# Closing one token tile four steps sooner, and the last inverse roots as one GpSimd power each, in a hybrid transformer block

## The chip, the cores and the metric

The kernel runs on one core of a Trainium2 chip. The metric is the device time of one execution in microseconds (us), the median of several. A core has TensorE (PE, matmuls), VectorE (DVE), ScalarE (ACT), GpSimd (POOL) and SyncE (SP, here only a queue that issues transfers). Each engine runs its own instructions in program order and waits on semaphores that the others raise.

## The reference, cut to what matters

512 tokens of width 1024 go through a gated block with attention and convolution, then through a retrieval layer over 16384 one-neuron experts, and a last layer norm. The change lies in the second half:

```python
# per token: 8 heads x 16 chosen experts with gates g
a = u_tab[experts] @ u2            # 128 dot products
y = sum(gelu(a) * g * v_tab[experts])
x = layer_norm(ALPHA * x + (1 + g2) * y, ln2_g, ln2_b)   # all in float32
```

## The kernel before

**Two ways for the tokens.** The tokens lie in four tiles of 128. For three of them (t = 0, 1, 2; TD = 3 of them) the gather over experts is done densely: for each of the CH = 128 groups of 128 experts, called steps here, PE multiplies a 128 x 384 matrix of weights by the group's 128 x 1024 rows of v_tab and sums in six PSUM banks (two halves of the width, three tiles). The fourth tile (t = TD) has its own 128 rows per token gathered by GpSimd's indirect transfers into a ring of 8 buffers (512 KB a row set), and DVE adds each to an accumulator in SBUF (`own_rows`, L1723). It has its own sum and norm (`own_sum`, `scales`).

**Split floats.** To keep float32 precision, every operand of PE is split into a high part (a copy by ACT in fp32r) and a low part (DVE's subtraction), and each product takes three matmuls. A step n is therefore this chain:

- SP loads rows of v (`load_v`) into one of DEEP = 5 buffers, once `low_v` of the step that had the buffer is done.
- ACT's `part_v(n)` makes the high part (L1039). The high parts have 5 buffers as well, so it waits for `v_mm`, the count of finished products, to reach n - 4 (product n-5 done). From step SIDE = 124 on the high and low parts lie elsewhere, in the space of the ring, and wait for the last own row only.
- DVE's `low_v(n)` makes the low part (L1688). DVE's `weigh(n)` makes the weights (L1676), ACT's `part_w(n)` their high part (L1026), DVE's `low_w(n)` their low part (L1683).
- PE's `second_product(n)` waits for `low_v(n)` and `low_w(n)`. It has 18 matmuls of 512 columns; from step 120 (CH - TAIL) only the 9 of the first half of the width. The 24 matmuls of each tile's second half for the last eight steps follow at the end, tile by tile.

**The order on DVE.** It is written out. In step n of the loop DVE does: `low_v` up to `low_target(n)`, then `weigh(n + 3)`, then as many own rows as OWN_AT[n] says, then `low_w(n + 2)`. ACT follows the same order with `part_v` and `part_w(n + 3)`. So `low_w(n + 2)`, for which PE waits, stands in DVE's queue behind every `low_v` of its step. The target is n + 4 until near the end:

```python
if n >= ROWS_TO + 2:
    return min(CH - 1, n + DEEP - 1 + (n - ROWS_TO - 1))
return n + DEEP - 1
```

`raw_target(n)` = `low_target(n)` + 5 tells SP how far to load. ROWS_TO, the step before which the own rows end, is 117 before the change. 98 of the 128 rows are spread evenly over the steps 46 to ROWS_TO - 1.

**The end.** DVE does `own_sum(0)` at the end of step 122, `own_sum(1)` at that of 124, and the norm of the own tile at that of 125. After the loop come, for each dense tile, `gated` (times the gate row, L1697), `last_sum` (L1704), statistics (L1106), `variances` (L1112, L1114), `centred` (L1139), the inverse root and `finished` (L1144). The inverse root is: ACT takes a square root (L797) while DVE does `centred`; then DVE takes the reciprocal and makes one Newton step (L1125 to L1129, five instructions), and for three of the tiles `shifts` (L1117). For the tiles TD and 1 the last operations go to others: ACT scales (L1075) and GpSimd adds the bias row (L777). GpSimd takes the first five inverse roots of the kernel as one power each (L682), at 11 us and between 374 and 392 us.

Of the kernel before, what the change touches and what calls it, by code (L numbers as in the profile page):

```python
# [9 lines left out]
ALU = mybir.AluOpType  # L10
ACT = mybir.ActivationFunctionType
# [6 lines left out]
TT = T // P  # L18
# [62 lines left out]
CH = NK  # L81
GR = 8
TD = TT - 1
# [28 lines left out]
TAIL = 8  # L112
# [6 lines left out]
W_STEP = BOTH - 5  # L119
GATE_STEP = BOTH + 5  # L120
EARLY_STEP = W_STEP // 2 + 2
ROWS_FROM, ROWS_EVEN, ROWS_TO = W_STEP, GATE_STEP + 5, CH - TAIL - 3
FIRST_ROWS = 4 * (BOTH - ROWS_FROM)
NORM_STEPS = tuple(range(DEEP_FROM + 9, DEEP_FROM + 21, 6))
XFIN_STEPS = tuple(range(DEEP_FROM + 21, DEEP_FROM + 21 + 6 * TT, 6))
# [45 lines left out]
def build(nc, x, ccol, w_modn, b_modc, w_modt, wblk, b_fc, conv_wc, conv_vec, keys_t, u_t, u_tab, v_tab, rows, out):  # L171
    with ExitStack() as ctx:
# [3 lines left out]
        def sb(name, shape, dt, kb):  # L176
            return nc.alloc_sbuf_tensor_at(name, shape, dt, offset=base + int(kb * KB))

        def sem(name):
            return ctx.enter_context(nc.semaphore(name))  # L180
# [58 lines left out]
        acc = sb("acc", [P, TT, D], F32, 184)  # L239
# [16 lines left out]
        xfin = sb("xfin", [P, TT, D], F32, 32)  # L256
        rows2 = sb("rows2", [P, 3, D], F32, 48)
# [7 lines left out]
        def small(name, shape, dt):  # L265
            n = 4
            for s in shape[1:]:
                n *= s
            t = nc.alloc_sbuf_tensor_at(name, shape, dt, offset=base + cur[0])
            cur[0] += (n + 31) // 32 * 32  # L270
            return t
# [11 lines left out]
        sq = small("sq", [P, 4, TT], F32)  # L283
# [49 lines left out]
        mask_r = sem("mask_r")  # L333
        cs_r = sem("cs_r")
        var_r = sem("var_r")
        dev_r = sem("dev_r")
        inv_r = sem("inv_r")
        xn_r = sem("xn_r")
        xT_mm = sem("xT_mm")
# [22 lines left out]
        xa_r = sem("xa_r")  # L362
# [4 lines left out]
        y_p = sem("y_p")  # L367
# [66 lines left out]
        class Chain:  # L434
# [5 lines left out]
            def link(self, ins):  # L440
                self.n += 1
                ins.then_inc(self.s, 1)
                self.eng.wait_ge(self.s, self.n)
# [42 lines left out]
        def w_parts(n):  # L486
            if O0 + 4 <= n < W0:
                return wo_hi[:, n - O0 - 4, :], wo_lo[:, n - O0 - 4, :]
            return (whi0, wlo0) if n == 0 else (whi[:, n % SPL, :], wlo[:, n % SPL, :])
# [179 lines left out]
        def _(pool):  # L669
# [102 lines left out]
                own_gather(j)  # L772

            pool.wait_ge(fin_in, 32)
            for i, t in enumerate((TD, 1)):
                pool.wait_ge(xa_r, 4 + i + 1)
                nc.gpsimd.tensor_tensor(xfin[:, t, :], acc[:, t, :], rows2[:, 2, :], ALU.add).then_inc(y_p, 1)  # L777


        @block.scalar  # L780
        def _(act):
            ch = Chain(act, ach)

            def hi(n):
# [6 lines left out]
                else:  # L791
                    need(act, blk_mm, n - SPL + 1 if n > SPL else 0)
                nc.scalar.activation(w_parts(n)[0][:, :], raw[:, s % RAW, :], ACT.Copy).then_inc(blk_hi, 1)

            def root(done, ts=slice(0, TT)):
                act.wait_ge(var_r, 5 + done)
                nc.scalar.activation(sq[:, 1, ts], sq[:, 0, ts], ACT.Sqrt).then_inc(dev_r, 1)  # L797

            def modulated(sh, sc, first, biased):

# [28 lines left out]
            for n in range(G0):  # L829
# [19 lines left out]
                elif n < V0 and (n - C0) % 2 == 1:  # L849
                    i = (n - C0) // 2  # L850
# [32 lines left out]
            for h in range(HEADS):  # L883
                n = G0 + 2 * h
# [79 lines left out]
            def part_u(c):  # L964
                act.wait_ge(u_in[c % RAW], 16 * (c // RAW + 1))
                need(act, u_mm, c - SPL + 1)
                nc.scalar.activation(whi[:, c % SPL, :], raw[:, c % RAW, :], ACT.Copy).then_inc(u_hi, 1)  # L967

            def gelu(c):
                m = c // 4  # L970
                act.wait_ge(u_mm, c + 1)
                if c >= SPILL + GS:
                    act.wait_ge(w_mul, c - SPILL - GS + 1)
                elif c == SPILL + PS:
                    act.wait_ge(sel_r, TT)
                elif c < SPILL + PS and c % 4 == 0 and m > 1:
                    act.wait_ge(gel_out[m % 2], 16 * (m // 2))
                nc.scalar.activation(gel_slot(c), bank[c % 2][:, 0:TN], ACT.Gelu_apprx_tanh).then_inc(gel_r, 1)
# [63 lines left out]
            for j in range(FILL):  # L1042
                ahead(SPILL + j)
                i = j - FIRST_W
# [9 lines left out]
            for n in range(CH):  # L1054
                if PRE + n - 1 < CH:
                    gelu(PRE + n - 1)
                if PRE + n + 2 < CH:
                    part_u(PRE + n + 2)
                while high_next <= low_target(n):
                    part_v(high_next)  # L1060
                    high_next += 1
                if n + 3 < CH:
                    part_w(n + 3)
                if n in (EARLY_STEP, W_STEP):
                    part = slice(0, SLOTS // 2) if n == EARLY_STEP else slice(SLOTS // 2, SLOTS)
                    act.wait_ge(dot_r, part.stop)
                    nc.scalar.activation(own_a[:, part], own_a[:, part], ACT.Gelu_apprx_tanh).then_inc(own_gel, 1)
                if n == CH - 3:
                    root(1, slice(TD, TT))
            for i, t in enumerate((TD, 0, 1, 2)):  # L1070
                if i:
                    root(1 + i, slice(t, t + 1))
                if t in (TD, 1):
                    act.wait_ge(scale_r, 4 + i)
                    nc.scalar.activation(acc[:, t, :], acc[:, t, :], ACT.Copy,  # L1075
                                         scale=sq[:, 2, t:t + 1]).then_inc(xa_r, 1)
# [3 lines left out]
        def _(dve):  # L1080
            ch = Chain(dve, dch)
            link = ch.link
            done = [0]
# [36 lines left out]
            def scales(last, roots, ts, meanwhile, shift=True):  # L1120

                variances(last, ts)
                link(meanwhile())
                dve.wait_ge(dev_r, roots)
                link(nc.vector.reciprocal(sq[:, 2, ts], sq[:, 1, ts]))  # L1125
                link(nc.vector.tensor_tensor(sq[:, 3, ts], sq[:, 2, ts], sq[:, 2, ts], ALU.mult))
                link(nc.vector.tensor_tensor(sq[:, 3, ts], sq[:, 3, ts], sq[:, 0, ts], ALU.mult))
                link(nc.vector.tensor_scalar(sq[:, 3, ts], sq[:, 3, ts], -0.5, 1.5, ALU.mult, ALU.add))
                link(nc.vector.tensor_tensor(sq[:, 2, ts], sq[:, 2, ts], sq[:, 3, ts], ALU.mult))  # L1129
                if shift:  # L1130
                    shifts(ts)

# [4 lines left out]
            def centred(dst, src, rows_of, t):  # L1137

                return nc.vector.scalar_tensor_tensor(out=dst[:, t, :], in0=src[:, t, :], scalar=mv[:, t, 0:1],  # L1139
                                                      in1=rows_of[:, 1, :], op0=ALU.subtract, op1=ALU.mult)  # L1140
# [106 lines left out]
            for n in range(G0):  # L1247
# [20 lines left out]
                elif n < V0 and (n - C0) % 2 == 1:  # L1268
                    i = (n - C0) // 2
# [34 lines left out]
            for h in range(HEADS):  # L1304
                n = G0 + 2 * h
# [394 lines left out]
            def last_sum(t, half):  # L1700

                cut = slice(half * HALF, (half + 1) * HALF)
                dve.wait_ge(pv_add, TD * half + t + 1)
                link(nc.vector.scalar_tensor_tensor(out=xfin[:, t, cut], in0=xfin[:, t, cut], scalar=ALPHA,  # L1704
                                                    in1=acc[:, t, cut], op0=ALU.mult, op1=ALU.add))
                return bn(xfin, t, half)
# [34 lines left out]
            for j in range(FILL):  # L1741
                low_u(SPILL + j + 2)
                i = j - FIRST_W
# [13 lines left out]
            for n in range(CH):  # L1757
                if PRE + n + 2 < CH:
                    low_u(PRE + n + 2)
                while low_next <= low_target(n):  # L1760
                    low_v(low_next)
                    low_next += 1
                if n + 3 < CH:
                    weigh(n + 3)
                for _ in range(DOT_AT[n]):
                    dot(next(dots))
                own_rows(n)
                if n + 2 < CH:
                    low_w(n + 2)
                if n in (EARLY_STEP + 1, W_STEP + 1):  # L1770
                    own_weights(int(n > W_STEP))
                if n == GATE_STEP:
                    dve.wait_ge(u_mm, CH)
                    diagonals(dg2, 40)
                if n == GATE_STEP + 3:
                    gate_row(rows2[:, 0, :], 0, 2)
                if n == CH - 6:
                    dve.wait_ge(fin_in, 32)
                    dve.wait_ge(x1_in, 16 * TT)
                    own_sum(0)  # L1780
                if n == CH - 4:
                    own_last = own_sum(1)
                if n == CH - 3:
                    scales(own_last, 1, ts=slice(TD, TT), meanwhile=lambda: centred(acc, xfin, rows2, TD))
            for t in range(TD):
                gated(t, 0)
            for t in range(TD):
# [1 line left out]

            for t in range(TD):  # L1790
                gated(t, 1)
                scales(last_sum(t, 1), 2 + t, shift=t < TD - 1, ts=slice(t, t + 1),
                       meanwhile=lambda: centred(acc, xfin, rows2, t))
                if t == 0:
                    finished(xfin, acc, rows2, t).then_inc(y_r, 1)
# [414 lines left out]
```

## Time and profile before

| | |
|---|---|
| median of 3 runs | 1601.46 us (1601.44 to 1603.22) |
| profiled execution | 1601.95 us |
| its span | 1600.1 us |
| PE busy | 1554.0 us (97%) |
| DVE busy | 1360.2 us (85%) |
| mean granted TensorE clock | 0.994 |

Busy is the time in which an engine worked on an instruction. Matmuls overlap, so a busy PE need not be at its peak. The span goes from the first to the last instruction on the core. The last 30 us of it hold the end of the loop, PE's three last groups of matmuls and the norms.

### The profile page before, as it was taken

The numbers are of one execution on the slowest core, as the hardware profiler recorded it, in microseconds if no ns is written. First come the engines' busy times: TensorE is split into PE (matmuls) and PEld (weight loads), VectorE is DVE, ScalarE is ACT, GpSimd is POOL, SyncE is SP. The second block draws the span as 40 slices with busy tenths as digits, with TensorE's granted clock in tenths as the row PEclk, the third lists the DMA queues.
The fourth block names the chain that finished last, engine by engine and source line by source line (L and its number), as shares of the span: only waits on it lengthen the run. The fifth ranks groups of instructions, "written<-read, shape, count | busy, mean of one in ns | idle before, by whom it ended". The sixth has DMA issues, their size and how long they took to land.

```text
span 1600.1 us, 21502 instructions
## 1 busy us (share of the span) xinstructions
PE 1554.0 (97%) x7776; PEld 1360.0 (85%) x7776; DVE 1360.2 (85%) x2580; ACT 677.4 (42%) x918; POOL 677.1 (42%) x451
## 2 busy tenths in 40 slices
PE   7999999997999999999999999999999999999996
PEld 4888777776899999999999999999998888878885
DVE  6579888696288899979994799999998899989988
ACT  4334656534433345554554433333333433333341
POOL 0201000001042878778764576666673344434401
PEclk9999999998999999999999999999999999999999
DMA  8423343562366666676778999999999999999961
GB/s 357 146 91 120 131 131 122 195 200 104 111 239 225 168 171 175 159 217 178 203 191 265 388 410 409 410 394 390 391 355 344 375 406 411 410 412 410 411 260 53
DMA packets 159753, 421.64 MB, mean 264 GB/s; under 512 B 31264, under 2 KB 64160, under 8 KB 159136
## 3 DMA queue, kind: packets, MB, share of 16 engines
q1 hardware_dynamic: 69552, 263.91, 44.7%
q0 software_dynamic: 57200, 139.58, 25.2%
q10 hardware_dynamic: 32896, 16.78, 3.8%
q8 instruction: 62, 1.02, 0.3%
q14 instruction: 43, 0.35, 0.1%
HBM read 375.03 MB, written 45.15 MB: 263 GB/s over the span
## 4 chain that ended last, share of the span: by engine, by line
PE 74%; DVE 19%; DMA 4%; issue 2%; ACT 1%; SPq 0%; DVEq 0%; POOL 0%; ACTq 0%
PE bank L1806 23%; PE bank L1808 23%; PE bank L1807 23%; DMA vraw<-in_v_tab_dram 3%; DVE one L1650 2%; DVE one L1648 2%; DVE wlo L1485 2%; DVE one L1652 2%; PE bank L1957 1%; PE bank L1942 1%; PE bank L2101 1%; PE bank L2077 1%; DMA modn<-in_w_modn_dram 1%; DVE eq L1588 1%; DVE acc L1723 1%
## 5 line engine op out<-in xcount | busy, mean ns | idle before, releaser
L1806 PE MATMUL bank<-act_hi,whi 128*128 128x384 f32 (+1 forms) x1352 | 481.2, 356 | 2.3 <-DVE act_lo L1207 1.5
L1807 PE MATMUL bank<-act_lo,whi 128*128 128x384 f32 (+1 forms) x1352 | 472.2, 349 | 0.0
L1808 PE MATMUL bank<-act_hi,wlo 128*128 128x384 f32 (+1 forms) x1352 | 472.1, 349 | 0.0
L1806 PE MATMUL bank<-vhi,eh 128*128 128x512 f32 x768 | 299.8, 390 | 3.8 <-DVE el L1683 3.7
L1808 PE MATMUL bank<-vhi,el 128*128 128x512 f32 x768 | 299.7, 390 | 0.0
L1807 PE MATMUL bank<-vlo,eh 128*128 128x512 f32 x768 | 299.7, 390 | 0.0
L1806 PEld LDWEIGHTS bank<-act_hi,whi 128*128 128x128 f32 x1352 | 255.1, 189 | 19.6 <-DVE act_lo L1207 2.1
L744 POOL DMA_INDIRECT gates_by_key<-selW,selS x128 | 238.3, 1862 | 69.3 <-issue 44.5
L1807 PEld LDWEIGHTS bank<-act_lo,whi 128*128 128x128 f32 x1352 | 255.2, 189 | 13.7
L1808 PEld LDWEIGHTS bank<-act_hi,wlo 128*128 128x128 f32 x1352 | 254.7, 188 | 13.4
L767 POOL DMA_INDIRECT ring<-in_v_tab_dram,idxN x128 | 168.8, 1319 | 203.0 <-DVE acc L1723 186.4
L728 POOL DMA_INDIRECT ring<-in_u_tab_dram,idxN x128 | 186.5, 1457 | 102.9 <-DVE ring L1490 59.6
L1688 DVE TENSOR_TENSOR vlo<-vraw,vhi 128x1024 fp32r<-128x1024 f32 x128 | 156.1, 1222 | 43.4 <-ACT vhi L1039 41.3
L1039 ACT ACTIVATE vhi<-vraw 128x1024 fp32r<-128x1024 f32 x128 | 135.2, 1058 | 127.6 <-PE bank L1808 114.7
L1485 DVE TENSOR_TENSOR wlo<-raw,whi 128x1024 fp32r<-128x1024 f32 x108 | 131.7, 1220 | 67.4 <-ACT whi L967 66.8
L1026 ACT ACTIVATE eh<-wf 128x384 fp32r<-128x384 f32 x128 | 67.4, 526 | 272.4 <-DVE wf L1676 272.4
L1806 PEld LDWEIGHTS bank<-vhi,eh 128*128 128x128 f32 x768 | 144.3, 188 | 34.9 <-issue 6.2
L1808 PEld LDWEIGHTS bank<-vhi,el 128*128 128x128 f32 x768 | 144.2, 188 | 30.2
L1807 PEld LDWEIGHTS bank<-vlo,eh 128*128 128x128 f32 x768 | 144.2, 188 | 29.3 <-issue 0.2
L1723 DVE SCALAR_TENSOR_TENSOR acc<-ring,own_a,acc 128x1024 f32<-128x1024 f32 x127 | 162.6, 1280 | 4.4
L1490 DVE SCALAR_TENSOR_TENSOR ring<-ring,x2s 128x1024 f32<-128x1024 f32 x128 | 150.0, 1219 | 4.1 <-DMA ring<-in_u_tab_dram,idxN 4.1
L967 ACT ACTIVATE whi<-raw 128x1024 fp32r<-128x1024 f32 x128 | 134.6, 1053 | 3.0 <-DMA raw<-in_u_t_dram 3.0
(256 smaller groups left out, 1903.3 us busy)
## 6 DMA issues: line engine op xcount, KB each, us to landing
raw<-in_u_t_dram SPq DMA_DIRECT2D x128, 512.0 KB, 7.1
vraw<-in_v_tab_dram SPq DMA_DIRECT2D x128, 512.0 KB, 9.7
raw<-in_wblk_dram SPq DMA_DIRECT2D x61, 512.0 KB, 4.4
gring<-gates_by_key SPq DMA_DIRECT2D x32, 768.0 KB, 12.4
raw<-in_w_modt_dram SPq DMA_DIRECT2D x32, 512.0 KB, 3.7
gates_by_key<-stage ACTq DMA_DIRECT2D x8, 2048.0 KB, 13.9
gelu_ahead<-gelz SPq DMA_DIRECT2D x20, 768.0 KB, 4.2
gback<-gelu_ahead SPq DMA_DIRECT2D x20, 768.0 KB, 17.1
```

Of the source, the lines that this page charges most:

```text
L728: pool.indirect_dma_start(out=ring[:, j % RING, :], out_offset=None, in_=u_tab, in_offset=bass.IndirectOffsetOnAxis(ap=idxN[:, j:j + 1], a ...
L744: pool.indirect_dma_start(out=gates_flat, out_offset=bass.IndirectOffsetOnAxis(ap=selS[:, n:n + 1], axis=0), in_=selW[:, n:n + 1], in_offs ...
L767: pool.indirect_dma_start(out=ring[:, j % RING, :], out_offset=None, in_=v_tab, in_offset=bass.IndirectOffsetOnAxis(ap=idxN[:, j:j + 1], a ...
L967: nc.scalar.activation(whi[:, c % SPL, :], raw[:, c % RAW, :], ACT.Copy).then_inc(u_hi, 1)
L1039: nc.scalar.activation(v_parts(n)[0], row, ACT.Copy).then_inc(v_hi, 1)
L1485: nc.vector.tensor_tensor(wlo[:, c % SPL, :], raw[:, c % RAW, :], whi[:, c % SPL, :].bitcast(F32), ALU.subtract).then_inc(u_lo, 1)
L1490: nc.vector.scalar_tensor_tensor(out=ring[:, j % RING, :], in0=ring[:, j % RING, :], scalar=1.0, in1=x2s[:], op0=ALU.mult, op1=ALU.mult, a ...
L1688: nc.vector.tensor_tensor(low, v_row(n)[0], high.bitcast(F32), ALU.subtract).then_inc(v_lo, 1)
L1723: nc.vector.scalar_tensor_tensor(out=acc[:, TD, :], in0=ring[:, j % RING, :], scalar=own_a[:, j:j + 1], in1=acc[:, TD, :], op0=ALU.mult, o ...
L1806: mm(o, wh, mh, start=start, stop=False)
L1807: mm(o, wh, ml, start=False, stop=False)
L1808: return mm(o, wl, mh, start=False, stop=stop)
```

## The change

ROWS_TO goes from CH - TAIL - 3 = 117 to 113. With it move the steps over which the own rows are spread (98 rows in 67 steps, not 71) and, through `low_target` and `raw_target`, the steps in which DVE, ACT and SP run further ahead: `low_target` is now 120, 122, 124, 126, 127 for the steps 115 to 119, where it was 119 to 122 for 115 to 118 and 124, 126, 127 for 119 to 121. `own_sum` is done in the steps 115 and 117 (122 and 124 before) and the own norm in 119 (125 before). The last four inverse roots are one GpSimd power each; ACT's square roots and DVE's five instructions are gone.

```diff
-ROWS_FROM, ROWS_EVEN, ROWS_TO = W_STEP, GATE_STEP + 5, CH - TAIL - 3
+ROWS_FROM, ROWS_EVEN, ROWS_TO = W_STEP, GATE_STEP + 5, CH - TAIL - 7
+OWN_SUMS, OWN_NORM = (ROWS_TO + 2, ROWS_TO + 4), ROWS_TO + 6
...
-            for i, t in enumerate((TD, 1)):
-                pool.wait_ge(xa_r, 4 + i + 1)
-                nc.gpsimd.tensor_tensor(xfin[:, t, :], acc[:, t, :], rows2[:, 2, :], ALU.add).then_inc(y_p, 1)
+            for i, t in enumerate((TD, 0, 1, 2)):
+                inverse_root(6 + i, slice(t, t + 1))
+                if t in (TD, 1):
+                    pool.wait_ge(xa_r, 4 + i // 2 + 1)
+                    nc.gpsimd.tensor_tensor(xfin[:, t, :], acc[:, t, :], rows2[:, 2, :], ALU.add).then_inc(y_p, 1)
...
-            def root(done, ts=slice(0, TT)):
-                act.wait_ge(var_r, 5 + done)
-                nc.scalar.activation(sq[:, 1, ts], sq[:, 0, ts], ACT.Sqrt).then_inc(dev_r, 1)
...
-                if n == CH - 3:
-                    root(1, slice(TD, TT))
             for i, t in enumerate((TD, 0, 1, 2)):
-                if i:
-                    root(1 + i, slice(t, t + 1))
...
                 variances(last, ts)
                 link(meanwhile())
-                dve.wait_ge(dev_r, roots)
-                link(nc.vector.reciprocal(sq[:, 2, ts], sq[:, 1, ts]))
-                link(nc.vector.tensor_tensor(sq[:, 3, ts], sq[:, 2, ts], sq[:, 2, ts], ALU.mult))
-                link(nc.vector.tensor_tensor(sq[:, 3, ts], sq[:, 3, ts], sq[:, 0, ts], ALU.mult))
-                link(nc.vector.tensor_scalar(sq[:, 3, ts], sq[:, 3, ts], -0.5, 1.5, ALU.mult, ALU.add))
-                link(nc.vector.tensor_tensor(sq[:, 2, ts], sq[:, 2, ts], sq[:, 3, ts], ALU.mult))
+                dve.wait_ge(inv_r, roots)
...
-                if n == CH - 6:
+                if n == OWN_SUMS[0]:
                     dve.wait_ge(fin_in, 32)
                     dve.wait_ge(x1_in, 16 * TT)
                     own_sum(0)
-                if n == CH - 4:
+                if n == OWN_SUMS[1]:
                     own_last = own_sum(1)
-                if n == CH - 3:
-                    scales(own_last, 1, ts=slice(TD, TT), meanwhile=lambda: centred(acc, xfin, rows2, TD))
+                if n == OWN_NORM:
+                    scales(own_last, 6, ts=slice(TD, TT), meanwhile=lambda: centred(acc, xfin, rows2, TD))
```

## Rows read from the trace of the kernel before

**Rows 1.** The page, busy time of each engine; then its group of own row additions.

```profile
PE 1554.0 (97%) x7776; PEld 1360.0 (85%) x7776; DVE 1360.2 (85%) x2580; ACT 677.4 (42%) x918; POOL 677.1 (42%) x451
...
L1723 DVE SCALAR_TENSOR_TENSOR acc<-ring,own_a,acc 128x1024 f32<-128x1024 f32 x127 | 162.6, 1280 | 4.4
```

**Rows 2.** The timeline of PE: start us, us, [idle before <-releaser]; products 92, 122, 123, last matmul.

```profile
1439.04 0.47 PE L1806 MATMUL bank<-vhi,eh 128*128 128x512 f32 x1 [1.01 <-DVE el L1683]
...
1558.48 0.47 PE L1806 MATMUL bank<-vhi,eh 128*128 128x512 f32 x1 [0.84 <-DVE el L1683]
...
1561.71 0.47 PE L1806 MATMUL bank<-vhi,eh 128*128 128x512 f32 x1 [0.94 <-DVE el L1683]
...
1588.15 0.39 PE L1808 MATMUL bank<-vhi,el 128*128 128x512 f32 x1
```

**Rows 3.** The timeline of ACT: high parts of v 122, then of 123 and 124.

```profile
1545.49 1.06 ACT L1039 ACTIVATE vhi<-vraw 128x1024 fp32r<-128x1024 f32 x1 [0.15 <-PE bank L1808]
...
1549.58 2.01 ACT L1039 ACTIVATE vhi<-vraw 128x1024 fp32r<-128x1024 f32 x2 [0.74 <-PE bank L1808]
```

**Rows 4.** The timeline of DVE, steps 119 to 125.

```profile
1550.67 2.36 DVE L1688 TENSOR_TENSOR vlo<-vraw,vhi 128x1024 fp32r<-128x1024 f32 x2 [1.92 <-ACT vhi L1039]
...
1555.04 2.36 DVE L1688 TENSOR_TENSOR vlo<-vraw,vhi 128x1024 fp32r<-128x1024 f32 x2 [1.07 <-ACT vhi L1039]
1557.31 0.55 DVE L1676 TENSOR_TENSOR wf<-gback,gring 128x384 f32<-128x384 f32 x1
...
1559.40 1.23 DVE L1688 TENSOR_TENSOR vlo<-vraw,vhi 128x1024 fp32r<-128x1024 f32 x1 [1.07 <-ACT vhi L1039]
...
1562.64 0.69 DVE L1731 TENSOR_TENSOR acc<-acc,rows 128x512 f32<-128x512 f32 x1
...
1564.70 0.54 DVE L1676 TENSOR_TENSOR wf<-gback,gring 128x384 f32<-128x384 f32 x1
...
1569.30 0.20 DVE L1112 BATCH_NORM_AGGREGATE mv<-stats 128x2 f32<-128x12 f32 x1
...
1569.61 1.27 DVE L1139 SCALAR_TENSOR_TENSOR acc<-xfin,mv,rows 128x1024 f32<-128x1024 f32 x1
...
1571.88 0.16 DVE L1117 SCALAR_TENSOR_TENSOR sq<-mv,sq 128x1 f32<-128x1 f32 x1
```

**Rows 5.** The timeline of DVE after the loop.

```profile
1573.75 2.57 DVE L1704 SCALAR_TENSOR_TENSOR xfin<-xfin,acc 128x512 f32<-128x512 f32 x1
...
1590.47 0.68 DVE L1697 TENSOR_TENSOR acc<-bank,rows 128x512 f32<-128x512 f32 x1
...
1592.95 2.27 DVE L1139 SCALAR_TENSOR_TENSOR acc<-xfin,mv,rows 128x1024 f32<-128x1024 f32 x1
...
1596.23 1.42 DVE L1144 SCALAR_TENSOR_TENSOR xfin<-acc,sq,rows 128x512 f32<-128x512 f32 x2
```

**Rows 6.** The timeline of GpSimd after the loop: its two bias additions.

```profile
1573.38 2.39 POOL L777 TENSOR_TENSOR xfin<-acc,rows 128x1024 f32<-128x1024 f32 x1 [50.25 <-ACT acc L1075]
...
1591.81 2.34 POOL L777 TENSOR_TENSOR xfin<-acc,rows 128x1024 f32<-128x1024 f32 x1 [16.04 <-ACT acc L1075]
```

**Rows 7.** Two powers on the timeline of GpSimd, and what DVE did during the second.

```profile
374.16 0.72 POOL L682 TENSOR_TENSOR sq<-sq,power 128x2 f32<-128x2 f32 x1 [89.00 <-DVE sq L1429]
...
384.95 1.66 POOL L682 TENSOR_TENSOR sq<-sq,power 128x2 f32<-128x2 f32 x1 [4.74 <-DVE sq L1429]
```

```profile
384.78 2.47 DVE L1416 SCALAR_TENSOR_TENSOR outg<-xres,mv,rows 128x1024 f32<-128x1024 f32 x2
```

**Rows 8.** Busy by window (PE, PEld, DVE, ACT, POOL, PEclk, DMA share, GB/s); DMA issues, KB, us to landing.

```profile
1400.00:1440.00 40.00, 38.87 (x170) 31.60 (x170) 35.46 (x42) 13.52 (x18) 15.79 (x13) 1.00 1.02 411
```

```profile
vraw<-in_v_tab_dram SPq DMA_DIRECT2D x9, 512.0 KB, 16.3
```

```profile
gring<-gates_by_key SPq DMA_DIRECT2D x32, 768.0 KB, 12.4
...
gback<-gelu_ahead SPq DMA_DIRECT2D x20, 768.0 KB, 17.1
```

More of the change, by code:

```diff
@@ L335, in build @@
         var_r = sem("var_r")
-        dev_r = sem("dev_r")
         inv_r = sem("inv_r")
@@ L1791, in _ @@
                 gated(t, 1)
-                scales(last_sum(t, 1), 2 + t, shift=t < TD - 1, ts=slice(t, t + 1),
+                scales(last_sum(t, 1), 7 + t, shift=t < TD - 1, ts=slice(t, t + 1),
                        meanwhile=lambda: centred(acc, xfin, rows2, t))
```

## The prediction

> **What bounds the kernel now.** I read the page first: PE is busy for 97% of the span [rows 1]. So time is won or lost where PE pauses, and after its last matmul. The waits of PE in the last 300 us are three, all for `low_w` on DVE (the instruction "el"): 1.01 us at 1439 us, before product 92, and 0.84 and 0.94 before the products 122 and 123 [rows 2]. Next the timelines of ACT and DVE, to see what stands ahead of "el". ACT starts the high part of v 122 at 1545.49 and that of 123 at 1549.58, each released by PE [rows 3]: one product takes 4.08 us, and the buffers of the high parts are the leash between PE and ACT. Last, the end: the last matmul starts at 1588.15 [rows 2] and DVE takes up its result only at 1590.47 [rows 5], 2.32 us later. A matmul (0.39 us) and a handover (0.1) make 0.49, so DVE is 1.83 us behind PE there; from 1559.40 on DVE has work nearly without a gap. The last 30 us are partly DVE's. Over the steps 46 to 116 the transfers are at their limit, too: the window at 1400 has the DMA engines busy all the time, at 411 GB/s, and a v load takes 16.3 us to land [rows 8].
>
> **What moves away from the end.** Two `own_sum` of 2.06 us (1562.64 to 1564.70) and a norm of 2.66 us (1569.30 to 1571.88 and 0.08 more) [rows 4] leave steps in which DVE is late, 6.8 us in all. That could win at most what DVE is behind at the end, 1.83 us, and little of PE's pauses: those before products 122 and 123 come from `low_v` in the steps 120 and 121, not from the sums.
>
> **What moves with ROWS_TO: the look-ahead.** This is the part that decides. `low_target` jumps by two from step 116 on. In step 116 DVE must do `low_v(121)` and `low_v(122)` before `low_w(118)`. ACT's `part_v(122)` waits for product 117 to end. But product 118 can't start without `low_w(118)`. So PE is idle from the end of 117 until a whole chain has run. In the kernel before, the same `low_v(122)` was in step 118, where `low_w(118)` had long been done, and the first pair (123, 124) was in step 119, behind which only `low_w(121)` stood. The chain in pieces, all from rows: product's last start to ACT's start 0.26; ACT's start to DVE's 1.09 (1549.58 [rows 3] to 1550.67 [rows 4]); a pair of `low_v` 2.27 (1555.04 to 1557.31), one of them 1.14; `weigh` to PE 1.17 (1557.31 [rows 4] to 1558.48 [rows 2]), of which 0.47 is `weigh`.
>
> - Product 118: 0.26 + 1.09 + 1.14 + 1.17 = 3.66 us of pause.
> - Product 119: step 117 has 123, which waits for product 118, and then 124. 0.26 + 1.09 + 2.27 + 1.17 = 4.79.
> - Product 120: `own_sum(1)` stands at the end of step 117, a pair in 118. From the start of `low_w(119)`: 0.47 + 2.06 + 2.27 + 1.17 = 5.97, against 0.70 + 4.08 = 4.78 at which PE is done with 119. Pause 1.19.
> - Product 121: PE's products are now half as long (2.04). From `weigh(121)` to `low_v(127)` is 2.09 (1557.31 to 1559.40 [rows 4]), then 1.14 and 1.17: 4.40, against 0.47 + 0.70 + 2.04 = 3.21. Pause 1.19.
> - Product 122: the own norm is at the end of step 119. With the norm at 2.26 (below): 0.47 + 2.26 + 0.05 + 1.17 = 3.95, against 2.74. Pause 1.21.
>
> Sum 12.04 us. Before, the pauses before 122 and 123 are 1.01 and 1.11 (the idle shown is 0.17 less each, since a matmul lasts 0.39 and the next may start after 0.23), and one before 125 is some 0.13: 2.25. All later `low_w` are ready in time. PE's last matmul comes 9.79 us later, at 1597.94. No pause is bridged: ACT, too, stands in `part_v` and nothing else feeds PE.
>
> **The inverse roots.** The power of 128 x 2 takes 0.72 us alone, but 1.66 when DVE had just begun an operation with two inputs in SBUF (384.78): it ended about 0.56 after DVE's first of the two [rows 7]. `centred` is such an operation, and it starts right behind the variance, so the power will come behind it. Before, `centred` to `shifts` is 2.27 us (1569.61 to 1571.88 [rows 4]). Then: 1.27 + 0.56 + 0.04 = 1.87. So a norm gains 0.40 us, not the 0.97 of the five instructions; bounds 0 (as now) and 0.97 (power hidden). The Trainium skill (SBUF — State Buffer, Who interferes with whom) says that a VectorE instruction with two SBUF inputs and a GpSimd one that reads SBUF exclude each other for the whole instruction. The rows agree; by it a norm gains 0.40 and the sum below stands, with the power at 0.72 alone it would be 0.6 less.
>
> The same is seen the other way round: GpSimd's addition (2.39 us from 1573.38, [rows 6]) stretches a 0.69 us sum on DVE to 2.57 [rows 5], to 0.55 after GpSimd's end, and the other (to 1594.15) stretches the last `centred` from 1.27 to 2.27. ACT's square root is on no path, and its removal is worth nothing: it lies under `centred`, which hides it.
>
> **The end of the span.** DVE is free when PE's last matmul ends, so the last `gated` starts at 1597.94 + 0.49 = 1598.43, 7.96 us later than before. From the last `centred` to `finished` it was 3.28 (1592.95 to 1596.23 [rows 5]), now 1.87: 1.41 won. But tile 1 now ends 5.44 us ahead of tile 2 (24 matmuls of 0.227), at 1592.99. Its `centred` starts 2.48 later (as 1590.47 to 1592.95), its scale is there after 1.87, and GpSimd adds 1.50 after that (1571.88 [rows 4] to 1573.38 [rows 6]): 1598.84. The last `last_sum` is due 0.7 after its `gated`, at 1599.14, falls into the addition and is held to 0.55 after 1601.23: 1.9 us lost. If it wins the race, the last `centred` is held instead, for 1.1. Bounds 0 and 1.9; I take 1.8. Span: + 7.96 - 1.41 + 1.8 = + 8.3 us.
>
> **The rows packed closer.** A step moves 512 KB of v, 192 KB each of gates and of saved gelus (768 KB in four steps [rows 8]), and 98/71 = 1.38 own rows of 512 KB (128 x 1024 floats [rows 1]): 1.64 MB, 402 GB/s at 4.08 us. With 98/67 = 1.46 rows it is 1.68 MB, 413 GB/s. The DMA engines give 411. The kernel before is close already: product 92 came 1.01 us late [rows 2], behind a v load, after the loads of x and of the norm's rows in the steps 54 to 84. By step 90 the new spread wants 3 more rows (65, not 62), 1.57 MB or 3.8 us of transfer, and 0.5 more by step 113. The end gives none of it back to PE. DVE's own load grows with it (0.08 rows of 1.28 us [rows 1]) and stays under 4.08. Bounds: 0, where the buffers take it, and 5 us. I take 3.3, since the buffers had nothing left at product 92, but some elsewhere.
>
> **Sum.** + 8.3 + 3.3 = + 11.6 us on the span of 1600.1. The profiled execution took 1601.95, 0.5 above the median of 1601.46; on the median it is 1613.1, 0.7% slower. One measurement of this kernel tells some 0.2% (3.2 us) from no change.
>
> **Rivals.**
>
> - *Only the look-ahead costs* (25%): the buffers swallow the denser rows. For it: one wait of 1 us in 290 us before; gathers have 8 buffers. Against it: 413 over 411. 1601.5 + 8.3 = 1609.8.
> - *The transfers cost in full or more* (20%): v loads arrive late again and again, and DVE, with only 0.16 us a step to spare, doesn't catch up. 1601.5 + 8.3 + 5 to 7 = 1615 to 1617.
> - *Faster* (5%): the pauses of 118 and 119 don't arise, as if `part_v(122)` didn't have to wait. Then the freed DVE wins its 1.83 and the 0.13 before product 125, and 1.41 of the root; with the late addition of GpSimd up to 1.8 lost: 1598.1 to 1599.9. And if the pauses before 122 and 123 went as well, 1596. It decides only if the new pauses together stay under some 3.5 us instead of 12; the release of that cast by PE is plain in [rows 3], which speaks against it.
> - *No change* (5%): pauses of 118 and 119 half as long and no transfer cost: 1601 to 1604.
> - My forecast has the rest, 45%; its own range is 1611 to 1615.
>
> All but one tenth is slower by more than 0.2%. The range that leaves two in ten out is 1607 to 1618: the look-ahead without GpSimd's collision and without transfers (+ 6), and with both in full.
>
> **What the new profile would show.** PE idle by some 3.5 and 4.6 us before products 118 and 119, released by "el", and three pauses near 1 us behind them; the cast of v 122 still released by PE; the power ending some 0.5 us after `centred`; the last `last_sum` or `centred` on DVE held by GpSimd's addition; and, in the steps 70 to 112, several PE waits for "el" behind v loads of 18 us and more. The prediction is wrong if PE runs through 118 and 119, or if the waits in the middle are absent or many times larger.

## The result, and the profile after

The changed kernel takes 1615.55 us (median of 4 runs, 1613.87 to 1616.35), against 1601.45 for the kernel before beside it: ratio 1.0088, 95% interval 1.0076 to 1.0099, so 14.1 us slower. The forecast was 1613.1, range 1607 to 1618. The profiled execution took 1615.5, its span is 1613.7 us, 13.6 more than before. In two of the experiments below one execution fell into a slow state (2232.18 us in experiment 2, 1733.01 in experiment 5); the ratios leave these two out.

In the changed kernel L1795 to L1797 are the matmuls, L1037 and L1677 the high and low part of v, L1665, L1024 and L1672 `weigh` and the high and low part of the weights. The timeline of PE (start us, duration us, idle us before and its releaser) shows ten pauses from step 46 on, all released by the low part of the weights. Six of them:

```profile
1390.45 0.47 PE L1795 MATMUL bank<-vhi,eh 128*128 128x512 f32 x1 [1.09 <-DVE el L1672]
...
1441.90 0.47 PE L1795 MATMUL bank<-vhi,eh 128*128 128x512 f32 x1 [1.27 <-DVE el L1672]
...
1552.74 0.76 PE L1795 MATMUL bank<-vhi,eh 128*128 128x512 f32 x1 [3.49 <-DVE el L1672]
...
1563.13 0.77 PE L1795 MATMUL bank<-vhi,eh 128*128 128x512 f32 x1 [4.63 <-DVE el L1672]
...
1571.62 0.47 PE L1795 MATMUL bank<-vhi,eh 128*128 128x512 f32 x1 [0.75 <-DVE el L1672]
...
1574.82 0.47 PE L1795 MATMUL bank<-vhi,eh 128*128 128x512 f32 x1 [0.88 <-DVE el L1672]
```

The third and the fourth are the products 118 and 119, which ran without a pause before. What stood ahead of their weights is seen on the timelines of ACT and DVE:

```profile
1549.34 1.06 ACT L1037 ACTIVATE vhi<-vraw 128x1024 fp32r<-128x1024 f32 x1 [3.02 <-PE bank L1797]
...
1558.60 2.00 ACT L1037 ACTIVATE vhi<-vraw 128x1024 fp32r<-128x1024 f32 x2 [5.91 <-PE bank L1797]
```

```profile
1550.43 1.22 DVE L1677 TENSOR_TENSOR vlo<-vraw,vhi 128x1024 fp32r<-128x1024 f32 x1 [2.81 <-ACT vhi L1037]
1551.57 0.55 DVE L1665 TENSOR_TENSOR wf<-gback,gring 128x384 f32<-128x384 f32 x1
1552.04 0.55 DVE L1672 TENSOR_TENSOR el<-wf,eh 128x384 fp32r<-128x384 f32 x1
1559.68 2.36 DVE L1677 TENSOR_TENSOR vlo<-vraw,vhi 128x1024 fp32r<-128x1024 f32 x2 [7.09 <-ACT vhi L1037]
1561.96 0.55 DVE L1665 TENSOR_TENSOR wf<-gback,gring 128x384 f32<-128x384 f32 x1
1562.43 0.55 DVE L1672 TENSOR_TENSOR el<-wf,eh 128x384 fp32r<-128x384 f32 x1
```

Read together: PE ends product 117 and releases the cast of v 122 (1549.34); DVE makes its low part (1550.43), then `weigh(119)`, then `low_w(118)` (1552.04), and PE starts product 118 at 1552.74. The same once more with a pair, 123 and 124, for product 119. The engines take turns: DVE is idle for 7.09 us while PE makes product 118 and ACT the cast that waited for it, then PE is idle while DVE makes two low parts and the weights. In the kernel before the cast of v 122 was followed by low weights that PE needed only much later [rows 3, 4].

The cast of v 122 also shows the middle of the kernel: it is at 1549.34, not 1545.49 [rows 3]. It is 3.85 us late before any of the tail's pauses.

The first matmul of each of the two products takes 0.76 and 0.77 us. The view by windows shows why (PE busy, PEld, DVE, ACT, POOL, the granted clock, DMA share, GB/s):

```profile
1549.00:1552.70 3.70, 0.25 (x2) 0.00 (x0) 2.16 (x3) 1.58 (x2) 0.00 (x0) 0.95 0.38 131
1552.70:1554.00 1.30, 1.26 (x3) 1.10 (x4) 0.00 (x0) 0.00 (x0) 0.00 (x0) 0.50 0.80 280
1554.00:1556.00 2.00, 2.00 (x6) 1.57 (x6) 0.00 (x0) 0.00 (x0) 0.00 (x0) 0.57 1.04 413
1556.00:1558.60 2.60, 2.50 (x11) 1.69 (x9) 0.00 (x0) 0.00 (x1) 0.00 (x0) 1.00 0.83 338
1558.60:1563.10 4.50, 0.00 (x0) 0.00 (x1) 3.42 (x5) 2.55 (x4) 0.00 (x0) 0.94 0.01 2
1563.10:1564.50 1.40, 1.37 (x3) 1.16 (x4) 1.33 (x3) 1.40 (x2) 0.00 (x0) 0.50 0.00 0
```

By the end of each pause the granted clock had gone to 0.50, the lower of its two levels (1.2 GHz, the other is 2.4), and it stayed there for about 3 us of matmuls (to 1555.8 in the first case). Product 118 took 5.60 us and 119 took 5.53 (from a product's first matmul to where the next product's would start, 0.23 after the last), where 4.08 is usual: 3.0 us that no step of the forecast has.

At the end, PE's last matmul, then the timelines of DVE and GpSimd:

```profile
1603.26 0.39 PE L1797 MATMUL bank<-vhi,el 128*128 128x512 f32 x1
```

```profile
1603.68 0.69 DVE L1686 TENSOR_TENSOR acc<-bank,rows 128x512 f32<-128x512 f32 x1 [0.89 <-PE bank L1797]
1604.41 2.54 DVE L1693 SCALAR_TENSOR_TENSOR xfin<-xfin,acc 128x512 f32<-128x512 f32 x1
...
1608.02 1.27 DVE L1128 SCALAR_TENSOR_TENSOR acc<-xfin,mv,rows 128x1024 f32<-128x1024 f32 x1
1609.81 1.41 DVE L1133 SCALAR_TENSOR_TENSOR xfin<-acc,sq,rows 128x512 f32<-128x512 f32 x2 [0.52 <-POOL sq L682]
```

```profile
1604.06 2.34 POOL L779 TENSOR_TENSOR xfin<-acc,rows 128x1024 f32<-128x1024 f32 x1 [1.53 <-ACT acc L1069]
1608.18 1.51 POOL L682 TENSOR_TENSOR sq<-sq,power 128x1 f32<-128x1 f32 x1 [1.78 <-DVE sq L1108]
```

GpSimd's addition begins 0.35 us ahead of DVE's last sum, which takes 2.54 us, not 0.69. The power ends 0.4 us behind `centred`, and DVE is idle for 0.52. From `centred` to `finished` it is 1.79 us, not 3.28 [rows 5].

### The profile page after: what moved, and what is told of

The parts are those of the page before. It is cut to its first block, busy times and chain, and to the rows that moved or that the text cites. A ratio compares the mean times of both kernels' runs of the same rounds, so it can differ in the third digit from the quotient of the medians.

```text
span 1613.7 us, 21481 instructions
## 1 busy us (share of the span) xinstructions
PE 1559.8 (97%) x7776; PEld 1363.1 (84%) x7776; DVE 1356.3 (84%) x2560; ACT 672.5 (42%) x913; POOL 687.7 (43%) x455
## 4 chain that ended last, share of the span: by engine, by line
PE 75%; DVE 17%; DMA 4%; issue 2%; ACT 1%; POOL 0%; SPq 0%; POOLq 0%; DVEq 0%; ACTq 0%
PE bank L1795 23%; PE bank L1797 23%; PE bank L1796 23%; DMA vraw<-in_v_tab_dram 3%; DVE one L1639 2%; DVE one L1637 2%; DVE wlo L1474 2%; DVE one L1641 2%; PE bank L2090 1%; PE bank L1946 1%; DVE acc L1712 1%; PE bank L1931 1%; PE bank L2066 1%; DMA modn<-in_w_modn_dram 1%; DVE wf L1665 1%
## 5 line engine op out<-in xcount | busy, mean ns | idle before, releaser
L1795 PE MATMUL bank<-act_hi,whi 128*128 128x384 f32 (+1 forms) x1352 | 482.1, 357 | 2.3 <-DVE act_lo L1196 1.5
L1797 PE MATMUL bank<-act_hi,wlo 128*128 128x384 f32 (+1 forms) x1352 | 473.2, 350 | 0.0
L1795 PE MATMUL bank<-vhi,eh 128*128 128x512 f32 x768 | 301.9, 393 | 14.1 <-DVE el L1672 13.9
L1797 PE MATMUL bank<-vhi,el 128*128 128x512 f32 x768 | 301.0, 392 | 0.0
L1795 PEld LDWEIGHTS bank<-act_hi,whi 128*128 128x128 f32 x1352 | 255.8, 189 | 19.6 <-DVE act_lo L1196 2.1
L1797 PEld LDWEIGHTS bank<-act_hi,wlo 128*128 128x128 f32 x1352 | 255.1, 189 | 13.4
L767 POOL DMA_INDIRECT ring<-in_v_tab_dram,idxN x128 | 173.9, 1359 | 185.6 <-DVE acc L1712 167.1
L1677 DVE TENSOR_TENSOR vlo<-vraw,vhi 128x1024 fp32r<-128x1024 f32 x128 | 156.1, 1221 | 51.8 <-ACT vhi L1037 50.8
L1037 ACT ACTIVATE vhi<-vraw 128x1024 fp32r<-128x1024 f32 x128 | 134.7, 1054 | 128.5 <-PE bank L1797 113.6
L1024 ACT ACTIVATE eh<-wf 128x384 fp32r<-128x384 f32 x128 | 67.4, 526 | 286.6 <-DVE wf L1665 286.6
L1795 PEld LDWEIGHTS bank<-vhi,eh 128*128 128x128 f32 x768 | 145.1, 189 | 47.9 <-issue 19.1
L1797 PEld LDWEIGHTS bank<-vhi,el 128*128 128x128 f32 x768 | 144.8, 189 | 30.3
## 6 DMA issues: line engine op xcount, KB each, us to landing
gring<-gates_by_key SPq DMA_DIRECT2D x32, 768.0 KB, 11.8
gates_by_key<-stage ACTq DMA_DIRECT2D x8, 2048.0 KB, 14.1
```

The source lines that it names most:

```text
L767: pool.indirect_dma_start(out=ring[:, j % RING, :], out_offset=None, in_=v_tab, in_offset=bass.IndirectOffsetOnAxis(ap=idxN[:, j:j + 1], a ...
L1037: nc.scalar.activation(v_parts(n)[0], row, ACT.Copy).then_inc(v_hi, 1)
L1677: nc.vector.tensor_tensor(low, v_row(n)[0], high.bitcast(F32), ALU.subtract).then_inc(v_lo, 1)
L1795: mm(o, wh, mh, start=start, stop=False)
L1797: return mm(o, wl, mh, start=False, stop=stop)
```

## The experiments

All ratios are against the kernel before, run on the same chip; its medians were 1600.65 us for experiments 1, 2, 4 and 5, 1601.05 for 3, 6, 7 and 8, and 1601.54 for 9 to 11.

**1. The look-ahead alone**, in the kernel before:

```diff
-    if n >= ROWS_TO + 2:
-        return min(CH - 1, n + DEEP - 1 + (n - ROWS_TO - 1))
+    if n >= 115:
+        return min(CH - 1, n + DEEP - 1 + (n - 114))
```

> The kernel before with nothing but the look-ahead moved: it begins at step 115, the own rows still end at 117, sums and norm stay in the steps 122 to 125. Theory (the look-ahead makes PE wait for a high part that waits for PE): product 118 waits some 3.7 us plus the two own rows that stand ahead of its low weights in step 116 (2.6), product 119 4.8, product 121 1.2; both long pauses are followed by slow products (1.4 us each, as in the profile after), and the 2.2 us of pauses before 122 and 123 and DVE's 1.8 us of lag at the end are absorbed: about 10 to 11 us, 1611 to 1612.5. Rival (the look-ahead is harmless, it is the sums and the norm put between the low parts that stop PE): no sum stands there in this kernel, so 1601 to 1602.

Measured: 1612.45 us, ratio 1.0071 (1.0058 to 1.0084), 11.8 us slower than 1600.65. The two pauses are there, the first longer by the two own rows that DVE does ahead of `low_w(118)`:

```profile
1551.96 0.77 PE L1806 MATMUL bank<-vhi,eh 128*128 128x512 f32 x1 [6.08 <-DVE el L1683]
...
1562.88 0.73 PE L1806 MATMUL bank<-vhi,eh 128*128 128x512 f32 x1 [4.63 <-DVE el L1683]
```

The two products behind them took 6.13 and 5.80 us, 3.8 us above the usual. So the look-ahead by itself stops PE; no sum or norm has been moved here. The rival falls.

**2. The rows closer, alone**, in the kernel before:

```diff
-          + spread(SLOTS - FIRST_ROWS - ROWS_EVEN + BOTH, n, ROWS_EVEN, ROWS_TO) for n in range(CH)]
+          + spread(SLOTS - FIRST_ROWS - ROWS_EVEN + BOTH, n, ROWS_EVEN, ROWS_TO - 4) for n in range(CH)]
```

> The kernel before with nothing but the own rows spread over the steps 46 to 112; look-ahead, sums and roots as before. Theory (transfers at their limit): PE waits more often for low weights in the steps 70 to 95, the cast of v 122 comes 3 to 4 us later than 1545.49, and 1604.5 to 1605.5 in all. Rival (the buffers take it, and the late cast in the profile after has another cause): 1601 to 1602.

Measured: 1605.22 us, ratio 1.0027 (1.0017 to 1.0037), 4.6 us by the medians, 4.3 by the ratio. PE has five pauses between 1390 and 1492, the longest 1.55 us, where it had one. The cast of v 122 is at 1549.12, 3.63 late:

```profile
1549.12 1.06 ACT L1039 ACTIVATE vhi<-vraw 128x1024 fp32r<-128x1024 f32 x1 [0.73 <-PE bank L1808]
```

**3. The same with lighter transfers.** Experiment 2, and of the saved gelus only the first of each four loaded (the engines' work stays as it is; the output isn't the reference's):

```diff
-                sp.dma_start(gback[:, q % 3], gel_dram[m]).then_inc(back_in[q % 3], 16)
+                sp.dma_start(gback[:, q % 3, 0:1], gel_dram[m, :, 0:1]).then_inc(back_in[q % 3], 16)
...
-                    src = gback[:, q % 3, c % 4, :]
+                    src = gback[:, q % 3, 0, :]
```

> The kernel before with the own rows closer, and with a quarter of the bytes of the saved gelus loaded (48 KB a step, not 192; all four steps of a group use the same quarter, so the output is not the reference's; the work of the engines is the same). Theory (the 4.6 us of the denser rows are transfer time): 1.54 MB a step are 377 GB/s, nothing waits for transfers, and the pause of 1 us of the kernel before goes too: 1599 to 1600.5. Rival (DVE with 31 steps of two rows, not 27, is what is late): 1604 to 1605.

Measured: 1598.85 us, ratio 0.9988 (0.9979 to 0.9997). All pauses of the middle are gone, those of the kernel before too; the two that are left in the trace after 1240 us are before products 122 and 123. In the same window as [rows 8], and the time a v load takes in it:

```profile
1400.00:1440.00 40.00, 40.00 (x178) 33.11 (x178) 38.29 (x45) 15.75 (x20) 19.66 (x16) 1.00 1.01 389
```

```profile
vraw<-in_v_tab_dram SPq DMA_DIRECT2D x10, 512.0 KB, 6.7
```

DVE has the same denser rows and is busier in this window than before (38.29 us against 35.46), and nothing is late. In the changed kernel a v load there takes 17.6 us. So the price of the denser rows is that of transfers, not of DVE's work.

**4. The powers alone**, in the kernel before:

```diff
-                dve.wait_ge(dev_r, roots)
-                link(nc.vector.reciprocal(sq[:, 2, ts], sq[:, 1, ts]))
...
+                dve.wait_ge(inv_r, roots)
...
+                inverse_root(6 + i, slice(t, t + 1))
```

> The kernel before with nothing but the last four inverse roots as GpSimd powers. Theory (a power has to wait until centred has let go and ends 0.5 us behind it, so each norm gains 0.4): all four norms lie in a stretch in which DVE is behind, 1.6 us in all, 1599.9. Rival A (the power is hidden, 0.97 per norm, of which 1.83 and 0.97 count): 1598.6. Rival B (GpSimd's addition for tile 1 is in its queue ahead of the last power and holds it up): 1601.5 or more.

Measured: 1598.83 us, ratio 0.9992 (0.9983 to 1.0), by the medians 1.8 us faster; the interval only just reaches no change. Each power takes 1.5 us and ends 0.4 us behind `centred`, near the 0.56 of the forecast. The last one stands in the queue behind GpSimd's addition and costs nothing by it, for `centred` is held up by the same addition.

**5. The changed kernel with its look-ahead back at step 119**:

```diff
-    if n >= ROWS_TO + 2:
-        return min(CH - 1, n + DEEP - 1 + (n - ROWS_TO - 1))
+    if n >= 119:
+        return min(CH - 1, n + DEEP - 1 + (n - 118))
```

> The changed kernel with the look-ahead alone put back to step 119. Theory: PE runs through 118 and 119, the pauses before 122 and 123 are back. Rows closer + 3.8, DVE no longer behind - 1.8 - 0.1, last root - 1.4, collision with GpSimd's addition + 1.8: 1603.7. Rival (the sums in the steps 115 to 119 are what stops PE): 1612 to 1615.

Measured: 1605.16 us, ratio 1.0025 (1.0016 to 1.0034). PE runs through 118 and 119. Against its own kernel before it is 4.0 us (by the ratio) to 4.5 us slower, where the terms of the expectation add up to 2.3. The trace shows 1.05 us of that: the pause before product 122 is 1.89 us, not 0.84, because the own norm, now at the end of step 119, holds up the pair of step 120. The rest is within the interval of the ratio.

```profile
1561.96 0.47 PE L1795 MATMUL bank<-vhi,eh 128*128 128x512 f32 x1 [1.89 <-DVE el L1672]
```

**6. The pauses filled.** The changed kernel, PE kept at work in them:

```diff
             def second_product(n, halves):
+                for _ in range({118: 17, 119: 22}.get(n, 0)):
+                    mm(bank[0][:, 0:P], ident[:], consts[:], start=True, stop=True)
                 pe.wait_ge(v_lo, n + 1)
```

> The changed kernel with matmuls into a bank that nobody reads put ahead of PE's waits for products 118 and 119 (17 and 22 of 128 x 128 in float32). The pauses stay, but PE isn't idle in them. If the slow first matmuls of 118 and 119 (1.4 us each beyond 4.08) come from the granted clock that fell in the idle, they go, and the pause before product 120, which they had covered, comes back with 1.2: 1.6 us less, 1613.9, and the clock is at 1.0 in the window from 1550 to 1566. Rival (they are slow for another reason, such as a transfer or an operand that is late): the time stays at 1615.5.

Measured: 1613.55 us, ratio 1.0082 (1.0069 to 1.0096), against 1.0088 of the changed kernel; as a difference of times that is not settled. The trace settles it: PE starts the extra matmuls at 1548.15, and product 118 at 1551.86, 3.71 later, as in the changed kernel (3.65). But the clock is at its upper level and the product takes 4.22 us, not 5.60:

```profile
1548.15 3.96 PE L2116 MATMUL bank<-consts,ident 128*128 128x128 f32 x34
1551.86 0.48 PE L1795 MATMUL bank<-vhi,eh 128*128 128x512 f32 x1
...
1556.08 5.07 PE L2116 MATMUL bank<-consts,ident 128*128 128x128 f32 x44
1560.90 0.48 PE L1795 MATMUL bank<-vhi,eh 128*128 128x512 f32 x1
...
1566.13 0.47 PE L1795 MATMUL bank<-vhi,eh 128*128 128x512 f32 x1 [0.88 <-DVE el L1672]
```

```profile
1551.00:1553.00 2.00, 2.00 (x15) 1.82 (x15) 0.66 (x2) 0.52 (x1) 0.00 (x0) 1.00 0.64 176
1553.00:1556.00 3.00, 3.00 (x15) 2.47 (x14) 0.00 (x0) 0.00 (x0) 0.00 (x0) 1.00 1.03 410
```

The last row of the first fence is product 120: its pause is back (0.88 us of idle). The slow clock of product 119 had hidden it. From the cast of v 122 to the end of the span it is 64.4 us in the changed kernel (1549.34 to 1613.7) and 63.0 here (1548.41 on ACT's timeline to 1611.4): 1.4 us, near the 1.6 expected.

**7. Tile 1's last operation on DVE**, in the changed kernel, ACT's scaling and GpSimd's addition for that tile taken out:

```diff
-                if t == 0:
+                if t < TD - 1:
                     finished(xfin, acc, rows2, t).then_inc(y_r, 1)
...
-                if t in (TD, 1):
+                if t == TD:
                     pool.wait_ge(xa_r, 4 + i // 2 + 1)
```

> The changed kernel with tile 1's last operation done by DVE in one instruction, as for tile 0, not by ACT's scaling and GpSimd's addition. Theory (the addition locks DVE's last_sum out for 1.85 us): that goes, and DVE's 1.28 us lie in the 0.9 us in which it waits for PE, so 0.3 to 0.4 are lost: 1.5 us less, 1614. Rival (the sum was late for another reason): 1615.5 to 1616.

Measured: 1612.6 us, ratio 1.0070 (1.0057 to 1.0084), 2.9 us less than the changed kernel by the ratios, where 1.5 was expected; the intervals of the two overlap a little. In the trace the last sum takes 0.69 again, and from the last `gated` to the end of the span it is 8.2 us (1606.02 to 1614.2), where it was 10.0:

```profile
1606.02 0.68 DVE L1686 TENSOR_TENSOR acc<-bank,rows 128x512 f32<-128x512 f32 x1
1606.74 0.69 DVE L1693 SCALAR_TENSOR_TENSOR xfin<-xfin,acc 128x512 f32<-128x512 f32 x1
```

The profiled execution was the slowest of the five, 1615.97 us, and it shows something more. PE pauses before 118 and 119 just as long as in the changed kernel (3.50 and 4.63 us), and this part of the program is the same, but matmuls stay at the slow pace of one in 0.43 us for 5.6 and 4.3 us, not 3. The two products take 6.78 and 6.18 us: 4.8 us above the usual, not 3.0. Product 118's last matmul, 119's first, and one that is still slow 3.5 us later:

```profile
1560.36 0.40 PE L1797 MATMUL bank<-vhi,el 128*128 128x512 f32 x1
1565.38 0.77 PE L1795 MATMUL bank<-vhi,eh 128*128 128x512 f32 x1 [4.63 <-DVE el L1672]
...
1568.93 0.63 PE L1797 MATMUL bank<-vhi,el 128*128 128x512 f32 x1
```

So what the slow clock costs behind the same pause differs from one execution to the next.

**8. The first sum early.** Rows (117) and look-ahead (119) as before, powers, and

```diff
+OWN_SUMS, OWN_NORM = (ROWS_TO, CH - 6), CH - 3
```

> A version meant to be faster: rows and look-ahead as in the kernel before (117, 119), own_sum(0) in step 117, where DVE waits for casts in the next two steps, own_sum(1) and the norm in 122 and 125 as late work, and the powers. Theory: no pause of PE is added; DVE catches up with PE before the last tile (- 1.8 - 0.1), the last root gives 1.4, and GpSimd's addition takes 1.8 back: 1599.2. Rival (any sum ahead of low parts costs PE its length): 1601 or more.

Measured: 1599.62 us, ratio 0.9991 (0.9982 to 1.0), 1.4 us faster where the terms of the expectation add up to 1.5; the interval only just reaches no change. As expected, no pause of PE is added in steps 117 to 127, DVE waits 0.88 us for PE at the last tile, and the last sum takes 2.54 us under GpSimd's addition.

**9. Experiments 7 and 8 together.**

> The version with the first sum in step 117, and tile 1's last operation on DVE as well. Theory (GpSimd's addition holds DVE's last sum for 1.85 us, and DVE's own instruction for it costs 0.2 after the 0.9 us in which it waits for PE): 1.6 us below the version with the first sum alone, about 3 us below the kernel before. Rival (the collision cost nothing at the end): 0.2 us above the version with the first sum alone.

Measured: 1597.37 us, ratio 0.9978 (0.9969 to 0.9987), 3.5 us by the ratio and 4.2 by the medians, faster than the kernel before by more than the noise. About 3 were expected.

**10. Weights first.** Experiment 9 with the look-ahead taken out and, from step 117 on, DVE's order turned round; sums in the steps 117 and 118, norm in 119:

```diff
-    if n >= ROWS_TO + 2:
-        return min(CH - 1, n + DEEP - 1 + (n - ROWS_TO - 1))
-    return n + DEEP - 1
+    return min(CH - 1, n + DEEP - 1)
...
-                while low_next <= low_target(n):
+                while n < ROWS_TO and low_next <= low_target(n):
                     low_v(low_next)
                     low_next += 1
...
                 if n + 2 < CH:
                     low_w(n + 2)
+                while low_next <= low_target(n):
+                    low_v(low_next)
+                    low_next += 1
```

> Rows until step 116 as in the kernel before, no look-ahead beyond n + 4 at all, and from step 117 on DVE does weigh and low_w ahead of low_v; sums in 117 and 118, own norm in 119, powers, tile 1's last operation on DVE. Theory (what stops PE is that its weights stand behind low parts it doesn't need yet): no pause of PE after step 117, so the 2.25 us before products 122, 123 and 125 go, DVE's lag of 1.8 goes, the last root gives 1.4, the tile 1 change costs 0.2: 5.3 us below before. Rival (the look-ahead is needed, since DVE has 2.08 us of work for a product of 2.04 and ACT's casts come in between): new pauses at the products 120 to 127, and 1600 or more.

Measured: 1595.18 us, ratio 0.9964 (0.9951 to 0.9976): 6.4 us below the kernel before by the medians, 5.8 by the ratio, where 5.3 were expected. It beats both kernels. After 1258 us PE waits for no weights at all; the last matmul starts four us earlier than before [rows 2]:

```profile
1584.18 0.39 PE L1798 MATMUL bank<-vhi,el 128*128 128x512 f32 x1
```

What the order and the earlier second sum and norm add to experiment 9 is less sure: 0.9964 against 0.9978 is 2.2 us, about the 2.25 us of pauses that are gone, but the two intervals overlap.

**11. The same order in the changed kernel**, whose rows end at 112 and whose sums are in the steps 115, 117 and 119:

> The changed kernel (rows until 112, sums in 115 and 117, norm in 119, powers), but no look-ahead beyond n + 4 and, from step 113 on, weigh and low_w ahead of low_v on DVE. Theory: the pauses before 118 to 122 go and only the denser rows' transfers (4.3 to 4.6) stay of the loss, against which stand - 2.25, - 1.8, - 1.4 and + 1.85 for GpSimd's addition: 1 us above before. Rival (the sums themselves stop PE when they are in the loop): 1610 or more.

Measured: 1600.76 us, ratio 0.9998 (0.9989 to 1.0007). From the changed kernel's ratio that is 1.0088 to 0.9998, or 14.4 us, by the order of DVE's instructions and the look-ahead alone. Putting the look-ahead back to step 119, experiment 5, gave 10.1 of it. The pauses of the middle are still there (six, up to 1.46 us). Experiment 10 is 5.6 us faster; its rows are spread as before, and it has tile 1's last operation on DVE as well.

## Why the prediction was right, and where it was off

**The look-ahead** was the step that decided, and it came as worked out. Counted from where the next matmul would have started, 0.23 us after the last one's start, the pause before 118 is 3.65 us (3.66 forecast) and that before 119 is 4.79 (4.79). The prediction calls its 0.26 us the time from the product's last start; from there it is 0.48 (1548.86 to ACT's 1549.34), and 0.26 is the time from where the next start would have been. Its sum is right all the same, for it gives the pause in the same count. The pauses before 121 and 122 are 0.91 and 1.05 (1.19 and 1.21). The one before 120 (1.19 forecast) didn't show, and experiment 6 shows where it was: behind product 119, slowed by the clock. Experiment 1 makes the pauses without the rest of the change, 5 and 11 take them away from it.

**What the sum lacked** is the clock: that one product takes 4.08 us was carried over from a PE that never rests to one that had just rested. Two products took 1.5 us more each in this profile, of which the pause before 120 that they covered takes back 1.2. PE's last matmul is at 1603.26, 15.1 us later; of this 3.85 are the middle and 11.26 the tail, where 9.79 were forecast. So of the 2.0 us by which the span exceeds the forecast (13.6 against 11.6) 1.5 are the tail (3.0 of slow clock, less 1.2 for the pause that it covered and 0.4 for two that came out shorter) and 0.5 the transfers. The medians differ by 14.1 us, 0.5 more. The 3.0 is what one execution shows: in the profile of experiment 7 the same two pauses are followed by 4.8 us of slow clock.

**The denser rows** were put at 3.3 us between bounds of 0 and 5; the profile has 3.85 (experiment 2 alone 3.6 in its profile and 4.3 to 4.6 in the medians). Experiment 3 shows that they are transfer time, and the rival in which the buffers take it all falls. That the size came out so well is in part luck. By step 90 the new spread wants 3 more rows (3.8 us at 411 GB/s), and product 92 was 2.86 us late (1441.90 against 1439.04 [rows 2]; 2.16 in experiment 2). But by the end of step 112 it is 98 rows against 92, six more, not the prediction's "0.5 more" than three: 3.1 MB, or 7.7 us at 411 GB/s. Half of that reached PE. What took the other half no run shows.

**The inverse roots**: 0.40 us per norm forecast, 0.5 measured (from the last `centred` 1.79, forecast 1.87, with no addition over it), not the 0.97 of the five instructions. Experiment 4 has the four of them at 1.8 us in all.

**GpSimd's addition** was expected to hold the last sum for 1.8 to 1.9 us: it is 1.85 (2.54 less 0.69), and experiment 7 takes it away. The Trainium skill (SBUF — State Buffer, Who interferes with whom) adds that the order of issue decides who blocks. The traces agree: before the change the addition began 1.34 us after the last `gated`, when the sum, due 0.7 after it, was under way, and it was `centred` that was held [rows 5, 6]; after the change GpSimd is first by 0.35 and holds the sum.

The measured time, 1615.55, lies where the rival "the transfers cost in full or more" had it. That rival wasn't the reason: the transfers took about 4, not 5 to 7, and the clock the rest. The rival "faster" needed PE to run through 118 and 119, and "no change" needed pauses half as long; both pauses came in full.

**Where the gain went.** The change moved 6.8 us of late DVE work away from the end, and DVE did catch up: at the last tile it waits 0.89 us for PE. The last `gated` starts 0.42 us after PE's last matmul, not 2.32, which is 1.9 us won, and the last root gives 0.5 (the other 1.0 of the 1.49 between `centred` and `finished` is the addition, which now holds the last sum for 1.85 in place of `centred`). Experiments 4 and 9 have such gains without the loss, 1.8 and 3.5 to 4.2 us. What ate them here was that ROWS_TO also steers the look-ahead and the spread of the rows.

What stays open: why experiment 7 gained 2.9 us where the end of its trace accounts for 1.8, within what the two intervals allow (the length of the slow clock, which differed between the two profiles, can move single executions by as much; the spread of either kernel's times was not taken apart); and whether the pause at 1258 us can be had back, which was not tried.

## What to carry to other kernels

A constant that says when one piece of work ends may also time others; list each of its uses before moving it, and for each ask which instruction now stands ahead of the one that the bottleneck waits for. Work done ahead costs nothing only as long as it can run: an early instruction that waits for the bottleneck's own progress, in the same in-order queue as what the bottleneck needs next, closes a ring. With the urgent instruction first the look-ahead wasn't needed: experiment 10, which has this, the early sums, the powers and tile 1 on DVE together, is 0.36% faster than the kernel before, 0.14% more than experiment 9 without it (the intervals of the two overlap).

And a pause of TensorE of some 4 us cost more than itself here: count the slow matmuls behind it, 1.5 to 2.7 us for each pause in the two profiles.

## What the runs showed of the hardware

- After 3.5 and 4.6 us of idle the granted clock was at 0.50, and matmuls were issued every 0.43 us in place of 0.23, for 3.1 and 3.0 us in the changed kernel's profile and for 5.6 and 4.3 in that of experiment 7. After pauses of 1 us (and, in experiment 5, one of 1.89) it stayed at 1.00. Matmuls whose result nobody reads kept it up.
- A GpSimd power of 128 x 1 took 1.5 us under DVE's `centred` and ended 0.4 us behind it, in the changed kernel and in experiment 4 each time; of the earlier ones of 128 x 2 those without such an operation ahead took 0.7 [rows 7].
- From 1280 to 1520 us the 16 DMA engines together moved 410 GB/s in the kernel before and 411 in the changed kernel and in experiment 2. Six more rows of 512 KB over some 270 us (by the prediction's estimate 413 GB/s of demand in place of 402) made PE 3.6 to 3.9 us late.
